# The last expert pair's down projection: six of eight rows of weights over all columns, two rows by column blocks, and result additions placed between scaling and low part

## The reference

```
gate, idx = lax.top_k(jnp.swapaxes(aff, 1, 2), cap)
xs = jax.vmap(lambda hb, ib: hb[ib])(h, idx)
a = jnp.einsum('becd,edf->becf', xs, w_gate)
u = jnp.einsum('becd,edf->becf', xs, w_up)
y = jnp.einsum('becf,efd->becd', jax.nn.silu(a) * u, w_down)
y = y * gate[..., None].astype(y.dtype)
return jax.vmap(lambda ib, yb: jnp.zeros((T, D), yb.dtype).at[ib.reshape(-1)].add(yb.reshape(-1, D)))(idx, y)
```

## Time and profile before

| | |
|---|---|
| Median of 3 executions | 1539.92 us (1539.81 to 1540.75) |
| Profiled execution, its own time | 1541.27 us |
| Its span (first to last instruction) | 1539.6 us |
| PE busy | 1451.0 us, 94% |
| PEld busy | 876.9 us, 57% |
| DVE busy | 602.1 us, 39% |
| ACT busy | 255.6 us, 17% |
| Moved by DMA | 572.46 MB, mean 372 GB/s |

### The profile page before, as it was taken

How to read it: one execution, slowest core, us unless ns; L and a number is a source line. 1 busy time by engine, 2 the same in 40 slices (tenths; PEclk the granted TensorE clock), 3 DMA queues, 4 the chain that set the end, 5 groups by cost and what they waited for, 6 DMA issues and landing times.

```text
span 1539.6 us, 18332 instructions
## 1 busy us (share of the span) xinstructions
PE 1451.0 (94%) x7752; PEld 876.9 (57%) x7752; DVE 602.1 (39%) x1019; ACT 255.6 (17%) x358; POOL 26.7 (2%) x58
## 2 busy tenths in 40 slices
PE   6899899999999999999989999999999899898997
PEld 2466579888899998435435335335335335335433
DVE  4433687788768987101301301301201201211313
ACT  4223123333234233000000000000000000000200
POOL 0000000000000000000000000000000000000000
PEclk7799899999999999999999999999999999999999
DMA  9999788876665687999999999999999999999999
GB/s 375 402 371 330 293 315 294 289 264 238 247 234 200 211 316 317 373 436 429 432 431 429 432 432 430 433 432 432 432 432 432 431 432 432 430 430 432 431 404 337
DMA packets 101870, 572.46 MB, mean 372 GB/s; under 512 B 9324, under 2 KB 56372, under 8 KB 80052
## 3 DMA queue, kind: packets, MB, share of 16 engines
q1 hardware_dynamic: 90432, 520.14, 83.1%
q0 software_dynamic: 6912, 50.33, 8.5%
q10 hardware_dynamic: 4468, 1.14, 0.3%
HBM read 565.02 MB, written 6.55 MB: 371 GB/s over the span
## 4 chain that ended last, share of the span: by engine, by line
PE 72%; DMA 24%; SPq 2%; DVE 1%; issue 1%; ACT 0%; POOL 0%; DVEq 0%; POOLq 0%
PE psum L609 70%; DMA ring<-in_w_up 19%; DMA ring<-in_w_ada 4%; DMA ring<-in_w_down 1%; SPq L519 1%; SPq L430 1%; PE psum L619 0%; PE psum L787 0%; PE psum L1027 0%; PE psum L997 0%; PE psum L750 0%; ACT mix L1202 0%; DVE hid L1819 0%; PE psum L642 0%; DVE hid L1818 0%
## 5 line engine op out<-in xcount | busy, mean ns | idle before, releaser
L609 PE MATMUL psum<-ring,hid 128*64 128x512 f32 x3024 | 685.1, 601 | 50.8 <-DMA ring<-in_w_up 35.6
L609 PEld LDWEIGHTS psum<-ring,hid 128*64 128x64 f32 x3024 | 244.0, 139 | 468.3 <-issue 414.6
L1889 DVE TENSOR_TENSOR hid<-psum,hid 128x512 f32<-128x512 f32 x16 | 11.1, 691 | 517.5 <-PE psum L609 517.5
L609 PE MATMUL psum<-h_parts,w_parts 128*128 128x384 f32 x1152 | 207.1, 337 | 0.0
L609 PEld LDWEIGHTS psum<-h_parts,w_parts 128*128 128x128 f32 x1152 | 200.0, 188 | 3.5 <-issue 2.5
L1453 DVE TENSOR_TENSOR w_parts<-ring,w_parts 128x2048 fp32r<-128x2048 f32 x52 | 119.0, 2289 | 88.0 <-ACT w_parts L1153 87.8
L1153 ACT ACTIVATE w_parts<-ring 128x2048 fp32r<-128x2048 f32 x52 | 99.6, 1915 | 224.3 <-PE psum L609 196.0
L609 PE MATMUL psum<-ring,early 128*32 128x512 f32 (+4 forms) x694 | 103.7, 582 | 19.2 <-DMA ring<-in_w_ada 18.0
L609 PE MATMUL psum<-w_parts,h_parts 128*128 128x512 f32 x432 | 108.2, 407 | 3.9 <-DVE h_parts L1497 3.9
L609 PEld LDWEIGHTS psum<-w_parts,h_parts 128*128 128x128 f32 x432 | 82.4, 195 | 33.0 <-issue 14.8
L609 PEld LDWEIGHTS psum<-early,mix 128*128 128x128 f32 x768 | 86.6, 192 | 9.0 <-issue 9.0
(11 more groups left out here) (214 smaller groups left out, 709.6 us busy)
## 6 DMA issues: line engine op xcount, KB each, us to landing
ring<-in_w_up SPq DMA_DIRECT2D x30, 4096.0 KB, 22.1
ring<-in_w_gate SPq DMA_DIRECT2D x28, 4096.0 KB, 29.3
ring<-in_w_down SPq DMA_DIRECT2D x26, 4096.0 KB, 29.8
ring<-in_w_ada POOLq DMA_DIRECT2D x48, 1024.0 KB, 6.9
ring<-in_w_in SPq DMA_DIRECT2D x36, 1024.0 KB, 7.6
ring<-in_w_ada SPq DMA_DIRECT2D x28, 768.0 KB, 15.4
res<-in_w_ada SPq DMA_DIRECT2D x16, 1024.0 KB, 5.0
ring<-in_w_out SPq DMA_DIRECT2D x16, 1024.0 KB, 5.4
```

The costliest lines, as they stand in the source:

```text
L609: return nc.tensor.matmul(out, lhsT, rhs, start=start, stop=stop, skip_group_check=True)
L1889: tt(by_row, bank[1][:, :].rearrange("p (b a) -> p a b", a=4), by_row, ALU.mult).then_inc(act_ready, 1)
```

## The change

The weights of the last downs are loaded and multiplied in another order. The first six of the eight row groups come as three full loads (`FULL = 3`, two row groups each) with all 2048 columns, one transfer of 2 MB an expert, each partition one run of 16 KB. They are accumulated into five banks that stay open (`down_full`). Only the last two row groups are loaded by column blocks, two rows a partition (`tail_load`, 10 transfers), and `down_tail` closes the five banks one after the other. Sends use a list of banks (`SENDS`), and a send waits for one addition that frees its bank. Block 4's down now stands ahead of block 3's send. On VectorE the additions of block b - 1 are woven into block b: one between scaling and low part, two behind it.

```
+FULL = 3
 TAIL = [(0, 512), (512, 512), (1024, 512), (1536, 256), (1792, 256)]
-TAIL_BANKS = [2, 3]
-SEND_BANKS = [[4, 5, 6], [7, 0, 1]]
+TAIL_BANKS = [2, 3, 6, 1, 4]
+SENDS = [5, 7, 0, 2, 5, 7, 0, 3, 2, 5, 7, 0, 6, 3, 2]
-TAIL_ORDER = [("d", 0), ("d", 1), ("s", 0), ("d", 2), ("s", 1), ("d", 3), ("s", 2), ("s", 3), ("d", 4), ("s", 4)]
+TAIL_ORDER = [("d", 0), ("d", 1), ("s", 0), ("d", 2), ("s", 1), ("d", 3), ("s", 2), ("d", 4), ("s", 3), ("s", 4)]
...
+            def down_pairs(e, part, sub):
+                first = (PAIRS - 1) * 2 * FF + e * FF + part * BLK
+                return down_rows[first:first + BLK, :].rearrange("(p j) n -> p j n", j=4)[:, 2 * sub:2 * sub + 2, :]
+
+            def full_load(n, e):
+                sp.dma_start(full_rows(n, e), down_pairs(e, n // 2, n % 2)).then_inc(moe_landed[n], 16)
+
+            def tail_load(b, e):
                 col, width = TAIL[b]
-                first = (PAIRS - 1) * 2 * FF + e * FF + half * BLK
-                src = down_rows[first:first + BLK, col:col + width].rearrange("(p j) n -> p j n", j=4)
-                sp.dma_start(tail_slot(b, e)[:, 4 * half:4 * half + 4, :], src).then_inc(tail_landed[b][half], 16)
+                sp.dma_start(tail_slot(b, e), down_pairs(e, 1, 1)[:, :, col:col + width]).then_inc(tail_landed[b], 16)
...
+            for n in range(FULL):
+                sp.wait_ge(moe_used, LAST + WIDE + n + 1)
+                for e in range(2):
+                    full_load(n, e)
+            sp.wait_ge(moe_used, LAST + 2 * WIDE)
             for b in range(len(TAIL)):
-                sp.wait_ge(moe_used, LAST + min(WIDE + b + 1, 2 * WIDE))
-                for half in range(2):
-                    for e in range(2):
-                        tail_load(b, half, e)
+                for e in range(2):
+                    tail_load(b, e)
...
+            def down_full(n):
+                pe.wait_ge(moe_landed[n], 48 * (PAIRS - 1) + 16 * (2 + 3) + 16)
+                for jj in range(2):
+                    for b, (col, width) in enumerate(TAIL):
+                        for e in range(2):
+                            mm(bank[TAIL_BANKS[b]][ES * e:ES * e + ES, 0:width], tail_rows(e, 2 * n + jj),
+                               full_rows(n, e)[:, jj, col:col + width], n == 0 and jj == 0, False)
+
+            def down_tail(b):
 
                 width = TAIL[b][1]
-                for f in range(FC):
-                    if f % 4 == 0:
-                        pe.wait_ge(tail_landed[b][f // 4], 32)
-                    for e, rows in enumerate((actT, actT1)):
-                        o = (f % 4) * P + (f // 4) * ES
-                        last = mm(out[ES * e:ES * e + ES, 0:width], rows[:, o:o + ES], tail_slot(b, e)[:, f, :], f == 0, f == FC - 1)
+                pe.wait_ge(tail_landed[b], 32)
+                for jj in range(2):
+                    for e in range(2):
+                        last = mm(bank[TAIL_BANKS[b]][ES * e:ES * e + ES, 0:width], tail_rows(e, 2 * FULL + jj),
+                                  tail_slot(b, e)[:, jj, :], False, jj == 1)
                 return last
...
+            for b in range(len(TAIL)):
+                y_scale(b)
+                if b:
+                    result(b - 1, range(0, 1))
+                y_rest(b)
+                if b:
+                    result(b - 1, range(1, NT))
+            result(len(TAIL) - 1, range(NT))
```

More of the change, by code:

```diff
@@ L336, in build @@
         moe_landed = [sem(f"moe_landed{n}") for n in range(WIDE)]
-        tail_landed = [[sem(f"tail_landed{n}_{half}") for half in range(2)] for n in range(len(TAIL))]
+        tail_landed = [sem(f"tail_landed{n}") for n in range(len(TAIL))]
         moe_used, half_used = sem("moe_used"), sem("half_used")
@@ L394, in build, with full_rows @@
         DRAINED = [[], [], [0], [1, 2], [3]] + [[s - 1] for s in range(5, U_OUT + 1)]
+        def full_rows(n, e):
+            return ring[:, WIDE_AT[n] + e, :].rearrange("p (j n) -> p j n", j=2)
         def tail_slot(b, e):
[L398 to L401, removed]
+            first, width = TAIL[b]
+            at = 4 * first + 2 * width * e
+            return ring[:, WIDE_AT[FULL] + at // SLOT, at % SLOT:at % SLOT + 2 * width].rearrange("p (j n) -> p j n", j=2)
         class Chain:
@@ L981, in down, with tail_rows @@
                 return last
-            def down_tail(b, out):
-                width = TAIL[b][1]
-                for f in range(FC):
-                    if f % 4 == 0:
-                        pe.wait_ge(tail_landed[b][f // 4], 32)
-                    for e, rows in enumerate((actT, actT1)):
-                        o = (f % 4) * P + (f // 4) * ES
-                        last = mm(out[ES * e:ES * e + ES, 0:width], rows[:, o:o + ES], tail_slot(b, e)[:, f, :], f == 0, f == FC - 1)
+            def tail_rows(e, f):
+                o = (f % 4) * P + (f // 4) * ES
+                return (actT, actT1)[e][:, o:o + ES]
+            def down_full(n):
[6 more added lines that the diff above has]
+            def down_tail(b):
+                width = TAIL[b][1]
+                pe.wait_ge(tail_landed[b], 32)
[3 more added lines that the diff above has]
+                                  tail_slot(b, e)[:, jj, :], False, jj == 1)
                 return last
@@ L1124, in send_last @@
                 pe.wait_ge(y_last, b + 1)
[L1125 to L1128, removed]
                 for t in range(NT):
-                    out, rows = bank[SEND_BANKS[b % 2][t]][:, 0:width], pickT[0][:, t * P:(t + 1) * P]
+                    n = NT * b + t
+                    if SENDS[n] in SENDS[:n]:
+                        pe.wait_ge(last_out, n - SENDS[:n][::-1].index(SENDS[n]))
+                    elif b == 0:
+                        pe.wait_ge(row_added, len(ROW_SENDS))
+                    out, rows = bank[SENDS[n]][:, 0:width], pickT[0][:, t * P:(t + 1) * P]
                     mm(out, rows, y_hi[:, first:first + width], True, False)
@@ L1140, in _ @@
             round_of(PAIRS - 1, last_pair=True)
+            for n in range(FULL):
+                down_full(n)
             for what, b in TAIL_ORDER:
@@ L1143, in _ @@
                     send_last(b)
-                    continue
-                down_tail(b, bank[TAIL_BANKS[b % 2]]).then_inc(moe_used, 1)
+                else:
+                    down_tail(b).then_inc(moe_used, 1)
         @block.scalar
@@ L1966, in y_tail, with y_rest, result @@
                 cols = slice(first, first + width)
-                stt(y_all[:, cols], bank[TAIL_BANKS[b % 2]][:, 0:width], slot_aff_last, g2_slots[:, cols], ALU.mult, ALU.mult).then_inc(tail_y, 1)
+                stt(y_all[:, cols], bank[TAIL_BANKS[b]][:, 0:width], slot_aff_last, g2_slots[:, cols], ALU.mult, ALU.mult).then_inc(tail_y, 1)
+            def y_rest(b):
+                first, width = TAIL[b]
                 v.wait_ge(tail_hi, b + 1)
+                cols = slice(first, first + width)
                 tt(y_lo[:, cols], y_all[:, cols], y_hi[:, cols].bitcast(F32), ALU.subtract).then_inc(y_last, 1)
-            def result(b):
+            def result(b, tiles):
                 first, width = TAIL[b]
-                for t in range(NT):
+                for t in tiles:
                     v.wait_ge(sent, 16 * (PAIRS - 2) + NT * b + t + 1)
                     rows = y_rows[:, t, first:first + width]
[L1976 to L1982, removed]
+                    tt(rows, bank[SENDS[NT * b + t]][:, 0:width], rows, ALU.add).then_inc(last_out, 1)
+            for b in range(len(TAIL)):
[6 more added lines that the diff above has]
+            result(len(TAIL) - 1, range(NT))
 def constants():
```

3 lines of the change are left out of this document (1 added, 2 removed).

## The result

The changed kernel took 1544.17 us in the median of 14 executions (1541.71 to 1547.31), the kernel before beside it 1540.92 (14 executions, 1539.08 to 1544.83). The ratio is 1.0023, 95% interval 1.0016 to 1.0031: slower by 3.3 us in the medians and 3.5 by the ratio. The forecast was 1542.3 in a range of 1540.3 to 1544.6 and put 64% on "within 0.2%"; the measured ratio lies just beyond that bound, and its interval takes in both sides of it. The kernel before was forecast from at 1539.92, the median of three executions, and stood at 1540.92 beside the changed one; 1.0 of the 1.9 us between forecast and measurement is that.

A forecast was written before the change was run, and what follows sets the result against it. Bound: the weight stream up to the last long-awaited landing, then PE, a VectorE chain and a store. Landing -3.2, landing to last addition +5.4, stores +0.2 gave +2.4 us: 1542.3 us, range 1540.3 to 1544.6.

The forecast's parts named there:

- within 0.2%: Whole kernel: time within 0.2%, 3.1 us, of the kernel before, from 1536.8 to 1543.0 us; chance 64%.
- term from landing to last addition: End of kernel: third full load's landing to VectorE's last addition takes 23.5 us where 18.1 stood, +5.4.
- store term: Final output stores: old 3.05 us from last addition to end, plus 0.2 because the last blocks' stores pile up.
- landing gain: Down-weight loads: third full load lands at 1515.25 instead of 1518.46, -3.2 us, from spacings of 9.75 us.
- Rival 1: PE's clock falls in the third row group after the second load wait: 1.6 us more, 1543.9, slower; 14%.
- slower: Whole kernel: time above 1543.0 us; chance 33%, summed from 14, 4, 9 and 6.
- the new limit: VectorE's chain on the last blocks: some 3.3 us per 512-column block, only 1.7 us of PE between blocks.
- the prediction's paragraph on row groups: PE on full loads: all 6.9 us of the third group stand behind its landing; before, only 3.4.
- 1.8 at most: VectorE's last blocks: additions between scaling and low part save ACT's 0.7 us idle for blocks 1 to 3, 1.8 at most.
- Rivals 2 to 5: Full rows no faster, +3.2 us, 4%; stores collide, 1-2.4, 9%; loads early, 1536.4, 3%; VectorE slack, 1-3 less, 10%.

The follow-up runs named there:

- e10_third_look: Changed kernel with no edit, run once more for a third profile; 1543.85 us, ratio 1.0025 to the kernel before.
- e2_fill: Changed kernel plus unused PE products behind the first and second full groups, filling PE's waits for loads; 1543.65 us, ratio 1.0020 to the kernel before.
- e6_short_runs: Changed kernel with each full load cut into four transfers of 512 columns, runs of 2 KB; ratio 1.0044 to the kernel before.
- e7_old_order: Changed kernel with VectorE doing scaling, low part, then all three additions of the block before, as before the change; ratio 1.0031 to the kernel before.
- e4_narrow: Changed kernel with eight of fifteen last additions cut to 64 columns, result incomplete; 1542.34 us, ratio 1.0017 to the kernel before.
- e5_by_group: Changed kernel with each full load split into its two row groups, own semaphores and runs of 8 KB; ratio 0.9996 to the kernel before.
- e9_wide_pair: Kernel before with sends moved into PE's waits, and blocks 0 and 1 as one 1024-column block, runs of 4 KB; 1538.55 us, ratio 0.9981 to the kernel before.
- after: First profile of the changed kernel itself, no further edit; median 1544.17 us, ratio 1.0023 to the kernel before.
- e1_again: Changed kernel with no edit, run a second time as the mark for the others; 1544.18 us, ratio 1.0021 to the kernel before.
- e3_two_full: Changed kernel with FULL = 2: four row groups in full rows, the last four by blocks, four rows a partition; ratio 0.9998 to the kernel before.

## Why the prediction came out as it did

**The structure held.** The third full load landed earlier than block 2's rows did before, PE never waited for a block's own load behind it, and VectorE was busy 12.43 of the 13.20 us from 1526.3 to 1539.5 and was last from block 3's scaling on. The term from landing to last addition was forecast at 23.5 us and was 23.5 in each profile of this order in which the clock stayed up in the third group (`e10_third_look`, `e2_fill`). The store term, forecast at 3.05 + 0.2, was 3.2 to 3.3 in the changed kernel and 3.5 in `e2_fill`.

**The landing gain was sized a little too large.** Forecast -3.2 us (29.25 from the last expert load); PE's start came 29.5 to 30.0 behind it, which leaves -2.5 to -3.0. The term was extrapolated as three equal spacings of 9.75, with the blocks' own short loads behind the third. In the five profiles of this order the second spacing was 9.7 and the third 9.85 to 10.4. The packets of the last 4.6 us ahead of the third start, 1510 to 1514.6 in the changed kernel, show what the extrapolation left out:

```profile
DMA packets 645, 1.75 MB, mean 381 GB/s; under 512 B 41, under 2 KB 41, under 8 KB 609
```

Nearly all of them are short: the blocks' own loads were already moving before the third full load was complete, at their lower rate. That is +0.4 us in the mean of the five profiles (+0.2 to +0.7).

**The clock was priced right, and its chance was too low by the prediction's own premises.** Rival 1 gave 1.6 us at 14%. Where it struck the changed kernel it cost 1.3 and 1.5 (24.8 and 25.0 against 23.5), and 1.7 in `e6_short_runs`. The step that went wrong is the weighing. With a wait of 2.9 us called "about even", and only the case counted in which the first wait is spared and the second is not, the chance is one in four, not 14%. Two of five profiles had it; five can't tell 25% from 40%. The other half of the argument, that a fall at the second group spares the third, held in `e10_third_look` and `e7_old_order` (waits cut to 1.63 and 1.05 us, full clock behind them) and not in `e6_short_runs`, where the slower loads left a wait of 2.26 and the clock fell in both groups. At two in five the clock adds some 0.5 us on average to the forecast of +2.4.

**Together** 2.4 + 0.4 for the landing + 0.5 for the clock is 3.3, and 3.3 (medians) to 3.5 (ratio) was measured; the agreement rests on the mean of five profiles. The chance of 33% for "slower" followed from a centre 0.7 us short of the bound; with these two terms right it would have been above one half. That 1544.17 still lies in the range of 1540.3 to 1544.6 is owed to the room left for the clock; that it lies near its upper end is owed to the 1.0 us by which the kernel before itself stood higher than in its first three executions.

**VectorE as "the new limit"** was right in order and too strong as a picture: PE stands 0.6 us behind it (`e4_narrow`). What set the time was how much PE work was tied to one late landing, 6.9 us, as the prediction's paragraph on row groups had it; `e5_by_group` took 3.5 us of it away by finer loads with a wait each. The gain from the order on VectorE, "1.8 at most", was 1.6 in the profile of `e7_old_order`.

**Rivals 2 to 5** did not come: short runs landed about 3 us later (`e6_short_runs`), the stores cost 0.1 to 0.4, no landing was earlier than 29.5 us.

**Left open:** the share of executions in which the clock falls at the third group (five profiles are few), what decides whether it falls after waits of the same length, and by how much the short loads delay the third landing in each execution, which varied by 0.5 us.

## What to carry to other kernels

Longer runs bring a transfer sooner (12.6 MB about 3 us sooner in runs of 16 KB than of 2 KB), but what the end sees is the landing plus all the work that one wait holds back: split the wait (row group by row group) before enlarging the transfer. Work that crosses all output blocks delays the first finished block; if each block still needs a chain on other engines, it should help to spread block completions at the pace of that chain, by the prediction some 3.3 us here; no run tests that pace by itself. After waits of 2.3 to 2.8 us on PE its clock fell in some profiles and not in others; the wait on the critical side should be kept shorter, and 1.3 us lost it in no profile here.

## What the runs showed of the hardware

Loads of this stage moved 347 GB/s in runs of 1 KB and 386 in runs of 2 KB, 407 in runs of 4 KB (`e9_wide_pair`), 420 in runs of 8 KB (`e5_by_group`), 421 in a stretch mostly of 16 KB runs (after) and 430 in the expert stage's largest packets: the rate still rises above 2 KB.

The clock fell after 2.60 us without work in `e10_third_look` and `e7_old_order` and held after 2.60 or 2.61 in four profiles (after, `e1_again`, `e4_narrow`, `e3_two_full`). It fell after 2.76 and 2.83 us (`e1_again`, after) and held after 2.78 (`e4_narrow`). The shortest wait that it fell after in these last 50 us is 2.26 us, in `e6_short_runs`, where the clock had been low early in the group before as well. After 1.63 us and less (`e10_third_look`, `e5_by_group`, `e7_old_order`, `e2_fill`) it held. So the length of the wait alone does not decide it.

Five open banks and a change of bank at every pair of products cost PE nothing: a step of 512 columns took 0.43 us (1517.80 to 1518.23), as in the earlier trace rows.
